# Layer 1 of a two-layer backbone: attention output products for tiles 2 and 3 moved into the first two expert heads, a new memory plan, and two late modulation chunks moved into the attention loop

## The reference

```python
hl = modulate(rmsnorm(xl, norm_g[i, 0]), sh1_l, sc1_l)   # 6 rows of silu(c) @ w_mod + b_mod
q, k, v = jnp.split(h @ w_in, 3, axis=-1)                # 12 chunks of 256 columns; rotary on latent q, k
a = p[:, :, 0] - lam_full * p[:, :, 1]                   # two softmaxes per head, 8 heads
o = rmsnorm(o, sub_g) * (1 - lam_init);  yl = o @ w_out
xl = xl + ga1_l * yl
hl = modulate(rmsnorm(xl, norm_g[i, 1]), sh2_l, sc2_l)
# peer_ffn: 8 heads, each: q = h @ w_q, scores to two sets of 128 keys, top 16 of 256 pairs,
#   16 experts: act = gelu(u[e] . h);  out += gate * act * v[e]
xl = xl + ga2_l * peer_ffn(hl)
return rmsnorm(xl, final_g)
```

## Time and profile before

| | us |
|---|---|
| median of three runs (3949.71 to 3957.34) | 3955.36 |
| the profiled execution | 3956.19 |
| its span, first to last instruction | 3954.4 |
| PE busy, share of the span | 3435.8, 87% |
| DVE busy | 2695.0, 68% |
| ACT busy | 1640.5, 41% |
| POOL busy | 1457.1, 37% |
| moved by DMA | 1462.16 MB, mean 370 GB/s |

### The profile page before, as it was taken

How to read it: one execution, slowest core, us unless ns; L and a number is a source line. 1 busy time by engine, 2 the same in 40 slices (tenths; PEclk the granted TensorE clock), 3 DMA queues, 4 the chain that set the end, 5 groups by cost and what they waited for, 6 DMA issues and landing times. The chain is left out here.

```text
span 3954.4 us, 36793 instructions
## 1 busy us (share of the span) xinstructions
PE 3435.8 (87%) x9512; PEld 1672.6 (42%) x9512; DVE 2695.0 (68%) x6302; ACT 1640.5 (41%) x4790; POOL 1457.1 (37%) x1321
## 2 busy tenths in 40 slices
PE   8978888888998989999999789888888888888886
PEld 4433433334444443445545464343334333333332
DVE  5867776768998887555554477547767767767765
ACT  3024444445555544533333305414444444444443
POOL 0034444434444434444444200024444444444442
PEclk9999999999999999999999998899999999999999
DMA  7389999999999999999999850159999999999997
GB/s 305 138 347 419 419 419 410 420 420 393 418 404 391 416 419 415 405 420 419 420 419 420 349 191 1 75 208 420 419 420 413 419 416 415 403 420 417 415 410 323
DMA packets 202627, 1462.16 MB, mean 370 GB/s; under 512 B 23088, under 2 KB 23472, under 8 KB 27056
## 3 DMA queue, kind: packets, MB, share of 16 engines
q0 software_dynamic: 189648, 1375.82, 84.7%
q1 hardware_dynamic: 12768, 84.00, 5.4%
HBM read 1457.63 MB, written 2.10 MB: 369 GB/s over the span
## 5 line engine op out<-in xcount | busy, mean ns | idle before, releaser
L1292 PE MATMUL ps<-arena 128*128 128x512 f32 x5120 | 2427.8, 613 | 423.5 <-ACT arena L1333 420.6
L1439 POOL DMA_INDIRECT arena<-experts,arena x1280 | 1437.1, 1123 | 2050.5 <-PE ps L1292 1782.6
L1364 DVE CUSTOM_DVE_ANT_0 arena<-arena 128x1024 f32<-128x1024 f32 x1280 | 1560.0, 1225 | 884.9 <-DMA arena<-experts,arena 877.3
L1292 PEld LDWEIGHTS ps<-arena 128*128 128x128 f32 x5120 | 929.0, 192 | 1744.9 <-ACT arena L1333 884.2
L1325 ACT ACTIVATE arena<-arena 128x1 f32<-128x1 f32 x1280 | 258.4, 202 | 1565.0 <-DVE arena L1364 1553.8
L1333 ACT ACTIVATE arena<-arena 128x128 f32<-128x128 f32 x1280 | 514.2, 402 | 93.0 <-issue 4.6
L1329 ACT ACTIVATE arena<-arena 128x1 f32<-128x1 f32 x1280 | 377.4, 295 | 90.0 <-issue 2.4
L1115 PE MATMUL ps<-arena 128*128 128x256 f32 x1280 | 289.6, 379 | 2.2 <-ACT arena L1261 2.2
L1115 PEld LDWEIGHTS ps<-arena 128*128 128x128 f32 x1280 | 241.9, 190 | 61.8 <-issue 30.2
L665 PE MATMUL ps<-arena 128*128 128x256 f32 x1024 | 234.6, 384 | 4.1 <-ACT arena L647 4.1
L665 PEld LDWEIGHTS ps<-arena 128*128 128x128 f32 x1024 | 197.1, 193 | 53.7 <-issue 24.6
(11 more groups left out here) (172 smaller groups left out, 2003.5 us busy)
## 6 DMA issues: line engine op xcount, KB each, us to landing
arena<-diff_w_in SPq DMA_DIRECT2D x24, 1024.0 KB, 9.1
arena<-experts,arena POOLq DMA_INDIRECT x1280
arena<-w_mod SPq DMA_DIRECT2D x16, 1024.0 KB, 4.9
arena<-w_late POOLq DMA_DIRECT2D x16, 1024.0 KB, 5.7
arena<-peer_wq SPq DMA_DIRECT2D x12, 1024.0 KB, 9.0
arena<-w_mod SPq DMA_DIRECT2D x4, 2048.0 KB, 17.9
arena<-w_early SPq DMA_DIRECT2D x8, 1024.0 KB, 9.5
arena<-b_mod POOLq DMA_DIRECT2D x12, 512.0 KB, 10.5
```

The source lines that it names most:

```text
L1292: last = nc.tensor.matmul(acc(t)[:, half * 512:(half + 1) * 512], diag[:, n % DIAGS, :], ring[:, n % SLOTS, D + half * 512:D + (half + 1) ...
L1364: nc.vector.tensor_tensor_reduce(out=u_row, in0=u_row, in1=h_of(t), scale=1.0, scalar=0.0, op0=ALU.mult, op1=ALU.add, accum_out=dots[:, j: ...
L1439: nc.gpsimd.indirect_dma_start(out=ring[:, n % SLOTS, :], out_offset=None, in_=experts, in_offset=bass.IndirectOffsetOnAxis(ap=idx_sb[:, u ...
```

## The change

1. **Tile 2 early.** Its normalisation, turn and copy for attention move into unit 44 of layer 0 (`LATER`). Only tile 3 is left at the layer change. The weights of chunk 2 get a place of their own and are loaded before the layer change; the first six steps are chunks 0 to 2 of tile 2, then of tile 3.
2. **Late chunks spread.** Six of the eight late chunks are summed one multiply-add at a time over 22 of the 24 steps, behind the rotation of each step. The sums of the last two stand in the attention loop, one multiply-add in each of units 8 to 23; their spreads stand behind the loop.
3. **Output products in halves.** `attention_out(pe, m, half)`: both halves of tile 0 and the first of tile 1 stand ahead of the first route, the second half of tile 1 behind it, tile 2's halves in unit 0 and tile 3's in unit 1 of layer 1. The waits for all four tiles on PE and POOL are gone. The second route's pair selection goes into unit 0.
4. **Memory.** The output weights of heads 6 and 7, the gain row and the temporary row leave the gather ring. Query weights get places that are free earlier: head 2 is loaded after the sums of squares, head 3 after the normalised outputs, heads 4 to 7 after the last output product.
5. **Final norm inside layer 1.** `last_act` and `last_dve` for tiles 0 to 2 stand in units 9, 17 and 25, for tile 3 behind the last unit; `last_norm` and its barrier are gone.

The diff, cut to its core:

```diff
-A_HT2_AT = 34536
+A_HT2_AT = 5120
+A_W2_AT = 34536
+A_XN3_AT = 48872
...
-A_WO2_AT = 48872
+A_WO2_AT = (9216, 11264)
+A_GAIN1_AT = 7168
 A_GA1_AT = 50920
-A_YTMP_AT = 51944
+A_YTMP_AT = 13312
...
+WQ_PLACES = ([20200 + 2048 * h for h in range(8)],
+             [20200, 22248, 34536, 4096, 24296, 26344, 28392, 30440])
...
+            if i == 1 and q == 1:
+                eng.wait_ge(sem("p_mm"), N_FIRST + 2)
...
+    def late_share(s):
+
+        return 48 * max(0, min(s - 1, 22)) // 22
+
+    def late_ready(j):
+
+        return min(s for s in range(len(STEPS)) if late_share(s) >= 8 * (j + 1))
+
+    def late_steps(dve, s):
+        for n in range(late_share(s - 1), late_share(s)):
+            late_one(dve, n)
+
+    def late_one(dve, n):
+        j, k, q = n // KD, n % KD, n // 4
+        w, a, c = late_weights(1, q)[:, k % 4, :], late_acc(1, j, 0), silu_c[:, k, 0:1]
+        if k % 4 == 0:
+            dve.wait_ge(sem(f"m1_late_w{q % 2}"), 16 * (q // 2 + 1))
+        if k == 0:
+            wait(dve, "m1_late_spread", j - 1)
+            last = nc.vector.tensor_scalar(a, w, c, None, ALU.mult)
+        else:
+            last = nc.vector.scalar_tensor_tensor(out=a, in0=w, scalar=c, in1=a, op0=ALU.mult, op1=ALU.add)
+        if k % 4 == 3:
+            last.then_inc(sem("m1_late_used"), 1)
+        last = dve.drain()
+        if k == KD - 1:
+            last.then_inc(sem("m1_late_sum"), 1)
...
-             + [(c, t) for c in range(12) for t in ORDER[4:]])
+             + [(0, 2), (1, 2), (2, 2), (0, 3), (1, 3), (2, 3)] + [(c, t) for c in range(3, 12) for t in ORDER[4:]])
...
+            if load == 14:
+                sp.wait_ge(sem("p_mm"), N_FIRST)
+                sp.dma_start(at(A_W2_AT, 2048), diff_w_in[2]).then_inc(sem("a_w2"), 16)
+                continue
...
+        if u == LATER and j == 10:
+            pe.wait_ge(sem("p_turn_out"), turned(N_FIRST))
+            token_turn(pe, 4, xn_first, xn_ps)
...
+        if u == LATER and b == 2:
+            act.wait_ge(sem("e0_x_out"), 5)
+            token_square(act, 2, xn_first)
+            token_roots(act, 2, 3)
+        if u == LATER and b == 6:
+            token_out(act, 4, 2, xn_ps)
...
     def attention_pe(pe):
-        for t in (2, 3):
-            token_turn(pe, t + 2, xn_last(t), xn_last_ps(t))
         for i in range(N_FIRST, len(STEPS)):
             step_product(pe, i)
+            if i == N_FIRST + 1:
+                token_turn(pe, 5, xn_last, xn_last_ps)
             if i > N_FIRST and STEPS[i - 1][0] < 8:
                 step_turn(pe, i - 1)
-            j = (i - N_FIRST - 4) // 2
-            if i % 2 == 0 and 0 <= j < LATE:
-                late_spread(pe, 1, j)
+            for j in range(LATE - 2):
+                if late_ready(j) + 1 == i - N_FIRST:
+                    late_spread(pe, 1, j)
+        late_spread(pe, 1, LATE - 3)
...
-        pe.wait_ge(sem("m1_late_read"), LATE)
+        pe.wait_ge(sem("m1_late_read"), LATE - 2)
...
+        late_spread(pe, 1, LATE - 2)
+        late_spread(pe, 1, LATE - 1)
...
-    def attention_out(pe, m):
-        if m == 0:
-            pe.wait_ge(sem("wo_in"), 32)
+    def attention_out(pe, m, half):
+        if (m, half) == (0, 0):
+            pe.wait_ge(sem("wo_in"), 48)
             pe.wait_ge(sem("t_onorm"), HEADS)
-        wait(pe, "t_y_out", m - 1)
-        for half in range(2):
-            for h in range(HEADS):
-                last = nc.tensor.matmul(out_ps(m)[:, half * 512:(half + 1) * 512], QT[:, m, h, :],
-                                        wo(h)[:, half * 512:(half + 1) * 512],
-                                        start=(h == 0), stop=(h == HEADS - 1))
-        last.then_inc(sem("t_y"), 1)
+            pe.wait_ge(sem("m1_late_read"), LATE)
+        if m >= 2 and half == 0:
+            pe.wait_ge(sem("t_y_out"), m)
+        for h in range(HEADS):
+            last = nc.tensor.matmul(out_ps(m)[:, half * 512:(half + 1) * 512], QT[:, m, h, :],
+                                    wo(h)[:, half * 512:(half + 1) * 512],
+                                    start=(h == 0), stop=(h == HEADS - 1))
+        if half:
+            last.then_inc(sem("t_y"), 1)
...
-            if 2 <= s < 2 + 2 * LATE:
-                late_sum(dve, 1, s - 2)
-            if s % 2 and 0 <= (s - 5) // 2 < LATE:
-                late_out(dve, 1, (s - 5) // 2)
             step_rotate(dve, i)
+            late_steps(dve, s)
+            for j in range(LATE - 2):
+                if late_ready(j) + 1 == s:
+                    late_out(dve, 1, j)
+        late_out(dve, 1, LATE - 3)
...
+            if 8 <= i < 8 + 2 * KD:
+                late_one(dve, 48 + i - 8)
+        late_out(dve, 1, LATE - 2)
+        late_out(dve, 1, LATE - 1)
+        nc.vector.tensor_copy(at(A_GAIN1_AT, D), at(A_GA1_AT, D))
...
+        OUT_HALVES = {(0, 4): (2, 0), (0, 11): (2, 1), (1, 3): (3, 0), (1, 8): (3, 1)}
...
+        def last_act(act, t):
+            W(act, "x_out", t + 1)
+            nc.scalar.activation(y_of(t), X[:, t, :], ACT.Square, accum_out=ssq[:, t:t + 1])
+            act.drain()
+            nc.scalar.activation(rstd[:, t:t + 1], ssq[:, t:t + 1], ACT.Sqrt, scale=1.0 / D, bias=eps
+                                 ).then_inc(sem("l_rms"), 1)
+
+        def last_dve(dve, t):
+            if t == 0:
+                dve.wait_ge(sem("final_g_in"), 16)
+            dve.wait_ge(sem("l_rms"), t + 1)
+            nc.vector.reciprocal(rstd[:, t:t + 1], rstd[:, t:t + 1])
+            dve.drain()
+            nc.vector.scalar_tensor_tensor(out=y_of(t), in0=X[:, t, :], scalar=rstd[:, t:t + 1], in1=at(LAST_G_AT, D),
+                                           op0=ALU.mult, op1=ALU.mult).then_inc(sem("l_done"), 1)
...
+                if layer and (u, j) in OUT_HALVES:
+                    attention_out(pe, *OUT_HALVES[u, j])
...
+                if layer and u // 8 > 0 and u % 8 == 1 and b == 0:
+                    last_act(act, u // 8 - 1)
...
+                if layer and (u, b) in ((1, 0), (1, 7)):
+                    attention_finish(dve, 2 + b // 7)
+                if layer and u // 8 > 0 and u % 8 == 1 and b == 5:
+                    last_dve(dve, u // 8 - 1)
...
-                if layer and n == 6:
-                    pool.wait_ge(sem("t_done"), LT)
...
-                    load_wq(sp, 7)
+                    load_wq(sp, 2)
+                    sp.wait_ge(sem("t_onorm"), HEADS)
+                    load_wq(sp, 3)
                     sp.wait_ge(sem("t_y"), LT)
-                    for h in range(2, 7):
+                    for h in range(4, 8):
                         load_wq(sp, h)
+                    sp.dma_start(at(LAST_G_AT, D), final_g.to_broadcast([P, D])).then_inc(sem("final_g_in"), 16)
+                    for t in range(LT):
+                        sp.wait_ge(sem("l_done"), t + 1)
+                        sp.dma_start(out[t * P:(t + 1) * P, :], y_of(t)).then_inc(sem("stored"), 16)
+                    sp.wait_ge(sem("stored"), 16 * LT)
...
-                    attention_out(pe, 0)
-                    attention_out(pe, 1)
+                    attention_out(pe, 0, 0)
+                    attention_out(pe, 0, 1)
+                    attention_out(pe, 1, 0)
                     turn_h(pe, 0)
                     q_product(pe, 0)
                     q_turn(pe, 0)
                     W(pe, "keys", 16)
                     key_product(pe, 0)
-                    attention_out(pe, 2)
+                    attention_out(pe, 1, 1)
                     q_product(pe, 1)
                     q_turn(pe, 1)
                     key_product(pe, 1)
-                    attention_out(pe, 3)
-                    pe.wait_ge(sem("t_done"), LT)
...
                     norm_dve(dve, 0)
+                    route_first(dve, 0)
                     attention_finish(dve, 1)
-                    route_first(dve, 0)
-                    attention_finish(dve, 2)
-                    route_first(dve, 1)
-                    attention_finish(dve, 3)
+                    first_keys(dve, 1)
+                    last_keys(dve, 1)
                     for u in range(units):
                         dve_unit(dve, u)
                     finish_tile(dve, tiles - 1)
+                    last_dve(dve, tiles - 1)
```

128 lines of the change are left out of this document (58 added, 70 removed).

## The result

The changed kernel takes 3926.3 us (median of 6 runs, 3922.8 to 3936.9) against 3955.9 before (6 runs, 3949.7 to 3957.9): ratio 0.9928, 95% interval 0.9915 to 0.9942, 29.6 us less, where 20.2 were forecast. The profiled span is 3923.6 against 3954.4, 30.8 less. Single runs of one kernel lie up to 20 us apart (17 of the kernel before, 3941.2 to 3961.1, in a later group), so the terms are read from the spans of stages in the traces.

What follows compares the result with a forecast made beforehand. DMA was taken to bound both long gather stages, a dependency chain the projections. Terms 2.5 - 21 + 6 + 2.9 - 6.4 + 3 - 7.2 = -20.2 us gave 3935 us, range 3922 to 3951 (forecast's own 3926 to 3945).

Steps and rivals of the forecast that it cites:

- 1, the end of layer 0: Layer 0's end: chunk 2's one-megabyte weight load delays the last landing and layer change by 2.5 us.
- 2, the projections: Barrier to third reduction: early tile 2 and thinner sums let PE set the pace; 21 us less despite a longer handover.
- the 96: Projections: PE's summed time in us, including 1.6 for half clock on first products and 2 for waits on late sums.
- 3, the loop's sums: Attention loop: sixteen late sums on DVE in units 8 to 23 cost 6 us, bounds 1.3 to 12.8.
- 4 and 5: Loop end to first gather: two spreads cost 2.9 us; one half product fewer ahead of the gather saves 6.4.
- 6 and 7: Layer 1: gather stream 3 us longer; end 7.2 us shorter with three of four Squares and outputs out of the tail.
- the +5 for final_g and three stores inside the stream: Gather stream: final_g and three of four stores, 2 MB, add 5 us of bytes.
- term 6: First gather to last landing: -5.7 + 2.5 + 5.2 + 1 = +3 us, bounds -3 and +24.6.
- A, the projections' pace: Rival: projections keep their 5 us a step, saving only 9 us there; 3947 us in all; chance 0.12.
- B, the sums in full: Rival: the attention loop pays its late sums in full, 12.8 us; 3942 us in all; chance 0.09.
- D: Rival: gather slots run dry by all 27.8 us of added products, stream +24.6; 3956.6 us in all; chance 0.07.
- C: Rival: PE falls to half clock in the attention loop, +43 us for all 16 units; 3978 us; chance 0.06.

Runs made afterwards that it cites:

- Experiment 6: The changed kernel with its 48 late sums beside the projections four a step, ahead of the rotation, as in the kernel before: 3947.7 us, ratio 0.9978.
- Experiment 3: The changed kernel with 8 of the loop's 16 late sums left out, those in units 1 and 2 of each head: 3927.8 us, ratio 0.9928.
- experiment 10: The changed kernel with the loop's 16 late sums in the 2nd and 3rd unit of each of the eight heads: 3925.2 us, ratio 0.9920.
- experiment 11: The changed kernel with projection sums over 20 steps, handover work moved, six filler products, loop sums mid-head, one half product before the first slot: 3912.2 us, 0.9889.
- Experiment 1: The changed kernel with the four half products of tiles 2 and 3 ahead of the first expert unit again: 3935.7 us, ratio 0.9944.
- Experiment 2: The changed kernel with the final norm as a block behind the last expert unit again, as before: 3931.3 us, ratio 0.9939.
- experiment 4: The changed kernel with a second, unused sum behind 12 of the 16 late sums in the attention loop: 3935.0 us, ratio 0.9944.
- experiment 12: The kernel before with six unused products on TensorE behind the scores of the loop's second unit: 3948.7 us, ratio 0.9981.

## Why the prediction was right

The sign and the range were right, though the narrower range of 3926 to 3945 held by only 0.3 us. The time came out 9 us below the forecast. In the profiles the difference is 10.6 us: 4.4 stand where no step of the sum was, the rest are misses of 0.8 to 2.2 us in every step, all but one of them the same way.

**1, the end of layer 0** (+3.5 against +2.5). The order of the loads is as forecast. In the twelve profiles that share this layer 0 the first product starts between 2242.3 and 2247.6, 2244.6 on the mean, against a barrier at 2240.4 and 2239.6 in the two of the old code: the step costs 4 to 5 us, two more than one megabyte in the full stream. Why was not tried.

**2, the projections** (-23.2 against -21). The mechanism is the forecast's: the first product is 0.17 us behind the barrier, the last copy 94.9 (96), steps are 3.67 apart, and the handover took 18.0 (18). Experiment 6 shows that the pace follows the number of sums in a step. Two costs in the 96 were mis-sized: the first products ran at full clock in this profile (7.14 for 32; 8.8 to 10.1 in nine of the eleven others), and the waits on late sums are one of 4.5 us on w_late.

**3, the loop's sums** (+4.3 against +6). The step "the two units without slack pay 0.8 each, 1.5 a head" failed in its size. Of the four heads with sums the first pays nothing (18.7), the next two 0.6 to 0.7 each (19.3), as does the head behind the last sum. Experiment 3 shows that the sums in units 1 and 2 of a head are free, experiment 10 that all sixteen cost under 1 us together, if they stand there (in a loop start at full clock they cost more, experiment 11). The other 1.7 of the 4.3 are one unit partly at half clock (6.85 us at 2456.78), which is gone with the sums of experiment 10, and stays with half of those in place. The condition that the forecast lacked is where in a head a sum stands: only that of the last unit costs.

**4 and 5** (-4.7 against -3.5). The two spreads cost 2.8 (2.9). The rest is 7.5 against 6.4: the turn is on h alone now, and PE's eight spreads of the roots take 12.78 us against 14.02. In both kernels the clock falls to half there, behind a wait of 4.1 us; here it fell after the first spread, in the kernel before ahead of it. The forecast has no such term. The changed kernel:

```profile
2531.00:2534.00 3.00, 2.74 (x5) 1.28 (x6) 1.11 (x3) 0.00 (x0) 0.00 (x0) 0.76 1.02 431
2534.00:2537.00 3.00, 3.00 (x4) 0.90 (x3) 1.33 (x2) 0.00 (x0) 0.00 (x0) 0.50 1.00 415
```

**6 and 7** (+1.6 against +3, -8.0 against -7.2). POOL's four waits are those of the forecast, and heads 0 to 2 together take as long as in the kernel before (132.9 against 132.7; 130.1 to 133.0 in nine profiles). Experiment 1 shows that this is not because the place is indifferent. Of the +5 for final_g and three stores inside the stream, experiment 2 shows 4.8: 3.1 behind the 48th gather, where the stores are, and 1.7 ahead of it, where final_g is loaded and where profiles differ by up to 2.9 anyhow. The sum for term 6 does not close as written (9 less 3.4 is 5.6, not 5.2, and its last +1 has no row); the total is off by less than 1 for it.

**What no step had: -4.4 at the loop's start.** The forecast took the half clock there as given. In six profiles of the same code up to this point, reduction 2 to 8 took 33.2, 33.2, 33.1 and 32.4 us, or 37.1 and 37.1 like the kernel before (37.6). In three of the short ones the clock came back early (pitch 3.87) and fell again, in the fourth it came back early and stayed. So up to 4 us of the 30.8 are luck, this state of the clock in one profile, and not the change's work.

**The rivals.** A, the projections' pace, is out (3.67). B, the sums in full, is out by experiments 3 and 10 (12.8 us against 4.3). D is out: the stream grew by 1.6. C did not come for the loop, but one unit at half clock is its mechanism on a small scale. By the Trainium skill ("TensorE: Matmul & The Clock Gate", A second HAM failure mode) the many small waits would swing the clock all through such a loop. The traces agree in a small part. Every profile with sums in units 8 to 23 has one to three short falls behind the loop's start (three with the twelve sums more of experiment 4), at a cost of up to 1.7 us each in the pitches. But the clock is 1.00 in between, and with the first wait filled the old loop, which has small waits and no sums, holds 1.00 to its end (experiment 12). So it is no swing all through, and the 43 us of C are far off.

## What to carry to other kernels

Read the granted clock ahead of each stage, not only within it: one wait of 2.4 us, with TensorE busy 1.6 of 4 us around it, cost 12 us in the units that followed, and six useless products gave some 8 of them back. When small work is moved beside a loop, look which of its iterations have the slack and put it there; the same sixteen sums cost 4 us, or under 1 us in the middle units of experiment 10. And where a stream is bound by DMA, what is moved inside it is paid by its bytes: an end shortened by 8 us was worth 3 to 5.
